# Making the low parts of the middle weight slots on GpSimd instead of VectorE in a two-layer attention/RWKV trunk

## What is computed

```python
for i in range(DEPTH):                       # DEPTH = 2
    p = x @ (w_in0 if i == 0 else w_in_rest[i - 1])
    p_att, p_gate = p[..., :N_ATT], p[..., N_ATT:N_ATT + N_GATE]
    p_rw = token_shift(p[..., N_ATT + N_GATE:N_IN0], mu_rwkv[i])   # r, k, v, w, a, g
    y_a = dsa_sparse_mqa(...)                # attention, 8 heads
    y_b = rwkv7_time_mix(...)                # a scan over time, 16 heads of 64
    g_a, g_b = jnp.split(jax.nn.sigmoid(p_gate + b_gate[i]), 2, axis=-1)
    x = layer_norm(alpha * x + (g_a * y_a + g_b * y_b) @ w_out[i], ...)
    x = layer_norm(alpha * x + conv_glu_ffn(x, ...), ...)
```

## Time and profile before

| | before |
|---|---|
| time, median of 3 runs | 1276.94 us (1275.41 to 1277.79) |
| time of the profiled execution | 1279.3 us |
| its span, first to last instruction | 1277.0 us |
| TensorE busy | 1183.0 us (93%) |
| VectorE, ScalarE, GpSimd busy | 768.0, 541.2, 53.7 us |
| mean granted TensorE clock | 0.981 of full speed |

### The profile page before, as it was taken

How to read it: one execution, slowest core, us unless ns; L and a number is a source line. 1 busy time by engine, 2 the same in 40 slices (tenths; PEclk the granted TensorE clock), 3 DMA queues, 4 the chain that set the end, 5 groups by cost and what they waited for, 6 DMA issues and landing times.

```text
span 1277.0 us, 28992 instructions
## 1 busy us (share of the span) xinstructions
PE 1183.0 (93%) x12328; PEld 1071.2 (84%) x12328; DVE 768.0 (60%) x1368; ACT 541.2 (42%) x954; POOL 53.7 (4%) x56
## 2 busy tenths in 40 slices
PE   7998999999989699999799989989999996999995
PEld 7778897978889599998597878979788996999984
DVE  0268565657457677774512775757584666777744
ACT  1343535354344255653112445354533443555530
POOL 0000000000000100000100000000000001000000
PEclk9999999999999799999999999999999998999998
DMA  7422221211175445555354222212111853555551
GB/s 261 149 87 88 84 87 45 88 51 60 52 250 169 158 157 189 183 195 201 114 193 148 84 75 67 93 52 92 40 47 52 275 174 129 188 180 193 199 187 43
DMA packets 45335, 165.35 MB, mean 129 GB/s; under 512 B 5120, under 2 KB 5376, under 8 KB 44960
## 3 DMA queue, kind: packets, MB, share of 16 engines
q1 hardware_dynamic: 42560, 154.01, 35.4%
q0 software_dynamic: 1504, 7.47, 1.9%
q10 hardware_dynamic: 1152, 2.10, 0.5%
HBM read 160.42 MB, written 3.15 MB: 128 GB/s over the span
## 4 chain that ended last, share of the span: by engine, by line
PE 78%; DVE 13%; ACT 3%; DMA 3%; issue 1%; POOL 1%; SPq 0%; POOLq 0%; DVEq 0%; ACTq 0%
PE ps L690 18%; PE ps L691 16%; PE ps L692 16%; PE ps L823 10%; PE ps L669 5%; PE ps L932 3%; DMA ring<-stream_dram 2%; PE ps L830 2%; DVE ring_r L1391 1%; DVE keep L1772 1%; PE ps L974 1%; DVE small L1770 1%; DVE ln L1635 1%; DVE X_Y L1501 1%; DVE x_tok L1632 1%
## 5 line engine op out<-in xcount | busy, mean ns | idle before, releaser
L690 PE MATMUL ps<-x_tok_r,mid_hi 128*128 128x256 f32 x448 | 137.0, 306 | 8.2 <-DVE ring_r L1391 8.2
L691 PE MATMUL ps<-xT_r,mid_hi 128*128 128x256 f32 x448 | 126.5, 282 | 0.0
L692 PE MATMUL ps<-x_tok_r,ring_r 128*128 128x256 f32 x448 | 126.3, 282 | 0.0
L669 PE MATMUL ps<-xT,ring 128*128 128x256 f32 x448 | 99.7, 381 | 0.0
L690 PEld LDWEIGHTS ps<-x_tok_r,mid_hi 128*128 128x128 f32 x448 | 85.1, 190 | 15.8 <-issue 8.4
L669 PEld LDWEIGHTS ps<-xT,ring 128*128 128x128 f32 x448 | 84.2, 190 | 13.0 <-issue 1.6
L691 PEld LDWEIGHTS ps<-xT_r,mid_hi 128*128 128x128 f32 x448 | 85.5, 191 | 0.0
L692 PEld LDWEIGHTS ps<-x_tok_r,ring_r 128*128 128x128 f32 x448 | 85.4, 191 | 0.0
L1391 DVE TENSOR_TENSOR ring_r<-ring,mid_hi 128x1024 fp32r<-128x1024 f32 x56 | 68.1, 1219 | 14.7 <-ACT mid_hi L1078 14.1
L1614 DVE TENSOR_TENSOR rs_ks_r<-ring,tha_kkn_r 128x1024 fp32r<-128x1024 f32 x46 | 56.4, 1225 | 25.2 <-ACT tha_kkn_r L1113 25.2
L1501 DVE COPY_PREDICATED X_Y<-masks,ps 128x256 f32<-128x256 uint32 x80 | 35.1, 438 | 60.0 <-PE ps L823 60.0
(11 more groups left out here) (427 smaller groups left out, 3361.4 us busy)
## 6 DMA issues: line engine op xcount, KB each, us to landing
ring<-stream_dram SPq DMA_DIRECT2D x281, 512.0 KB, 3.3
lora_w<-lora_dram POOLq DMA_DIRECT2D x2, 1536.0 KB, 7.2
W_bt<-rpar_dram POOLq DMA_DIRECT2D x4, 512.0 KB, 4.7
kt_V<-rpar_dram POOLq DMA_DIRECT2D x4, 512.0 KB, 6.0
x_tok<-x_dram SPq DMA_DIRECT2D x2, 512.0 KB, 4.6
v_saved_dram<-vs_dC ACTq DMA_DIRECT2D x4, 256.0 KB, 3.6
x_tok<-x_dram SPq DMA_DIRECT2D x1, 1024.0 KB, 5.0
vf<-v_saved_dram ACTq DMA_DIRECT2D x4, 256.0 KB, 3.5
```

Source lines behind the costliest of these rows:

```text
L669: mm = pe.matmul(dst[:, b, :], w[:, kb * P:kb * P + P], rhs[:, kb, :], start=(kb == 0), stop=(kb == KB - 1))
L690: pe.matmul(dst, lh, rh, start=start, stop=False)
L691: pe.matmul(dst, lh, rl, start=False, stop=False)
L692: return pe.matmul(dst, ll, rh, start=False, stop=stop)
```

## The change

The low parts of the middle slots are made by GpSimd. The semaphore is `pool_mid` in place of `dve_mid`. GpSimd makes them in the order in which TensorE reads them; its small steps are placed among them by gap: `y_rstd(r - 1)` after the slots of gap 2, `head_norm(r + 1)` after those of gap 13. VectorE's five calls of `mids_up_to` go. TensorE waits for `xr` by itself before middle slot 0.

```diff
@@ gpsimd
+            def mids_up_to(l, end):
+                for m in range(pool_mid.next - l * MID_PER_LAYER, min(end, MID_PER_LAYER)):
+                    k = SLOT_AT[MIDS[l * MID_PER_LAYER + m]] % RING
+                    pool.wait_ge(*act_mid(l, m))
+                    pool.tensor_tensor(rounded["ring"][:, k, :], ring[:, k, :], f32(mid_hi[m % NM][:, :]), ALU.subtract
+                                       ).then_inc(*pool_mid.inc(l, m))
+            def y_rstd(r):
+                pool.wait_ge(*dve_y(r, "v8"))
+                pool.tensor_scalar(g8[:, 3, :], g8[:, 2, :], 1.0 / N_R, GN_EPS, ALU.mult, ALU.add
+                                   ).then_inc(*pool_y.inc(r, "eps"))
+                pool.wait_ge(*pool_y(r, "eps"))
+                pool.tensor_tensor(g8[:, 4, :], g8[:, 3, :], half[:, 0:NU], ALU.pow
+                                   ).then_inc(*pool_y.inc(r, "rstd"))
@@ gpsimd, the rounds
                 for g in range(GROUPS):
                     r = GROUPS * l + g
+                    mids_up_to(l, mids_by(GAPS * g + 2))
+                    if g:
+                        y_rstd(r - 1)
+                    mids_up_to(l, mids_by(GAPS * g + 13))
                     if g + 1 < GROUPS:
                         head_norm(r + 1)
-                    pool.wait_ge(*dve_y(r, "v8"))
-                    pool.tensor_scalar(g8[:, 3, :], g8[:, 2, :], 1.0 / N_R, GN_EPS, ALU.mult, ALU.add
-                                       ).then_inc(*pool_y.inc(r, "eps"))
-                    pool.wait_ge(*pool_y(r, "eps"))
-                    pool.tensor_tensor(g8[:, 4, :], g8[:, 3, :], half[:, 0:NU], ALU.pow
-                                       ).then_inc(*pool_y.inc(r, "rstd"))
+                    mids_up_to(l, mids_by(GAPS * g + 13 + 2 * (NCH - 1)))
+                y_rstd(r)
@@ tensor, pair_pieces
-                        pe.wait_ge(*dve_mid(l, m))
+                        if m == 0:
+                            pe.wait_ge(*dve_parts(l, "xr"))
+                        pe.wait_ge(*pool_mid(l, m))
@@ vector
-            def mids_up_to(l, end):
-                for m in range(dve_mid.next - l * MID_PER_LAYER, min(end, MID_PER_LAYER)):
-                    k = SLOT_AT[MIDS[l * MID_PER_LAYER + m]] % RING
-                    dve.wait_ge(*act_mid(l, m))
-                    dve.tensor_tensor(rounded["ring"][:, k, :], ring[:, k, :], f32(mid_hi[m % NM][:, :]), ALU.subtract
-                                      ).then_inc(*dve_mid.inc(l, m))
@@ vector, grams / level / after grams / after each chunk
-                if r % GROUPS:
-                    mids_up_to(r // GROUPS, mids_by(GAPS * (r % GROUPS) - 1) - 1)
-                mids_up_to(r // GROUPS, mids_by(GAPS * (r % GROUPS) + 2))
-                    mids_up_to(r // GROUPS, mids_by(GAPS * (r % GROUPS) + 1 + 2 * lev + k))
-                    mids_up_to(l, mids_by(GAPS * g + 3))
-                        mids_up_to(l, mids_by(GAPS * g + 13 + 2 * c))
```

More of the change, by code:

```diff
@@ L451, in trunk @@
         act_mid = by_layer("act_mid", list(range(MID_PER_LAYER)))
-        dve_mid = by_layer("dve_mid", list(range(MID_PER_LAYER)))
+        pool_mid = by_layer("pool_mid", list(range(MID_PER_LAYER)))
         mid_last = mid_gaps()
```

## The result

The changed kernel takes 1288.1 us (median of 9 runs, 1285.05 to 1298.68), the kernel before 1277.7 us beside it (9 runs, 1273.16 to 1281.96). The ratio is 1.0088 with an interval of 1.0062 to 1.0113: slower, by 11.2 us, with 7.9 and 14.4 as bounds. Forecast were +3.8 us. The side and the cause (VectorE held while GpSimd subtracts) were as forecast; the size was not.

What follows compares the result with a forecast made beforehand. TensorE, 78% of the chain, plus its waits bounds the kernel. Two layers lose 4.4 us and slot 0 gives -0.6: +3.8 us, median 1280.7 us; the forecast's own range is 1276 to 1290, 8-in-10 range 1265 to 1293.

Steps and rivals of the forecast that it cites:

- Price of a low part: One subtraction on GpSimd was taken as 2.25 us, within bounds of 1.2 and 3.1 us.
- Held both ways: GpSimd's subtraction holds VectorE's operations with two SBUF inputs, just as they hold GpSimd; forecast case at 0.45 chance.
- first rival: VectorE is not held, so only gains remain: -10.9 us, 1266.0 us; chance 0.28.
- Chunks: Chunk 1 of each round and the last round's chunk 2: S held, 0.49 us lost each, 2.45 a layer.
- Level 3: Rounds 1 and 2: subtraction leaves the chain ahead of the second X update, 1.0 us gained twice a layer.
- y_scale: Level 2 of rounds 1 and 2: L1566 held by slot 12's subtraction, 0.2 us lost each, 0.4 a layer.
- starts of rounds 1 and 2: GpSimd's subtraction holds L1480, which TensorE reads 0.3 us late in each of these rounds.
- slot 0 of layer 0: xr starts 1.7 us late, less the 1.15 of the removed subtraction: 0.55 us lost.
- the start of round 3: Held L1480 makes Y start 0.75 us late with no middle slots as cover: 0.75 us lost a layer.
- The clock: Forecast is wrong if TensorE's granted clock falls in the last round's longer pauses; no size in the sum.
- Slot 0 of layer 1: GpSimd is done before xr, so the removed subtraction gains 1.15 us.
- third rival: A low part takes 2.65 us or more and VectorE is held longer: +15 us, 1292, up to 1304; chance 0.10.

Runs made afterwards that it cites:

- fills: Changed kernel with each GpSimd subtraction replaced by two fills of the same tile that read nothing, low parts zero: 1266.74 us, ratio 0.9892.
- one-wait kernel: Changed kernel with GpSimd starting slot 24 only after VectorE is through with akrk of round 3: 1285.83 us, ratio 1.0052 to the kernel before.

## Why the forecast held in sign and not in size

- **Price of a low part.** Taken 2.25 us, measured 2.37. The Trainium skill (GPSIMD Engine Reference, Elementwise — side-by-side cycle accounting) gives 4497 ns for 2048 elements, as an estimate 2.25 us for half; the trace has 5% more. By the forecast's own slope (3.8 us at 2.25, 15 at 2.65) the 0.12 us would have brought 3.4 us more, 7.2 in all. The places do not show it: the ten in the chunks, where a longer subtraction should tell, came out below the forecast.
- **Held both ways.** Shown: S waits for the subtraction's end in all 16 places of the group (chunks 1 and 2), and does not beside fills. The first rival (no holding) is out, and so is its ground, the 1.23 us at 358.97: there GpSimd's instruction reads 8 elements.
- **Chunks.** 0.49 forecast, 0.37 measured: 1.2 us too much over ten places. In chunk 2 of rounds 0 to 2 S is held as well, and the cover that I had named is there: they moved by nothing.
- **Level 3, y_scale, starts of rounds 1 and 2, slot 0 of layer 0.** -0.91 for -1.0, 0.16 for 0.2, 0.32 for 0.3, 0.61 for 0.55. xr now takes 4.06 us from 113.11, by the end of the second subtraction.
- **The step that failed: the start of round 3, put at 0.75 us a layer.** It measured 2.9 in both, without the clock. I followed the held L1480 to its end and let L1486 and Y run behind it at their usual length. But the hold itself moves what follows into the next slot's subtraction: the second half of L1486 waits too, and Y comes about 3 us late. The groups show that this happens at every start: L1495 has 14.7 us more than before ((1398 - 479) ns x 16), which is seven pairs at 2.1 us, the three round starts of each layer and slot 0 of layer 1. In rounds 1 and 2 the middle slots cover it, as I had said; in round 3 there is nothing to cover with. The runs with slot 24, slot 25 and both settle it: by the matmuls 0.82, 0 and 2.94 us a layer. The 0.75 was right for the one hold that I had followed; the hold behind it was missing.
- **The clock.** Named as what could go wrong, and not in the sum. TensorE's products behind the 2.82-us pause run at 0.50 of full clock in layer 0. The two falls in that stretch give away 2.6 us there (1.5 of it right behind the pause, the rest at 320.9) and 1.7 in layer 1. How much of that is the change's stays open. In layer 1 the same pause of 2.82 us is followed by the same products in 1.15 us, at full clock, and the fall comes 1.1 us after they begin; with slots 24 and 25 alone layer 1 has one only 8.4 us after, as the kernel before has. In layer 0 six profiles of kernels without the two holds in a row also have a spell of half clock, 8.6 to 9.9 us after these products begin, and the kernel before and three others have none. So the second fall of layer 0 is not of this change alone; the first, right behind the pause, stands in the two kernels with both holds and in no other. Each kernel was profiled once, and no run here holds the clock fixed.
- **Slot 0 of layer 1, -1.15 forecast.** I had only looked whether GpSimd is done before xr, which it is. Its first subtraction catches L1495 before Y, by the same pair pattern (VectorE's timeline after; the two took 0.88 us before):

```profile
745.69 2.98 DVE L1495 SCALAR_TENSOR_TENSOR tmp<-rs_ks,cpar 128x256 f32<-128x256 f32 x2
748.84 0.74 DVE L1520 COPY_PREDICATED X_Y<-masks,ps 128x512 f32<-128x512 uint32 x1 [0.17 <-PE ps L840]
```

  The gain was there (-1.18 us), and the hold took 1.47 (read in the one-wait kernel's profile, which has no half clock at this place): +0.3, and the rest is a half-clock spell at 744. The kernel in which slot 0 waits for this step has the gain alone.
- **Level 4 of round 0, not in the forecast.** Four tensor_scalar operations of att_norm take 3.16 us beside slot 4 instead of 1.01 (137.79), 0.29 us a layer. I had counted only operations with two SBUF inputs as held.

The sum with these terms: 3.8, + 4.4 for round 3 (2 x 2.2 more), + 1.45 for slot 0 of layer 1, + 0.6 for level 4, - 1.2 for the chunks, + 0.4 for the level 3 gains: 9.4 us before any clock. That lies within the measured 7.9 to 14.4; the 1.8 us to the 11.2 may be clock, or nothing.

That 1288.1 us still lies within the forecast's own 1276 to 1290 is luck in part: the sum was let move with the price of a low part alone, and that price was nearly as taken. By the time alone the third rival (1292 us, at 2.65 us a low part) was nearer to it than the forecast's 1280.7; the measured 2.37 us and the holds in a row speak against that rival.

## What to carry to other kernels

Before work goes to GpSimd, walk along VectorE's queue at each place and ask which instruction meets the new one, then redo the walk from the delayed times, because one hold can push the next instruction into the next hold. Give GpSimd what lies beside VectorE instructions that take one of their inputs from PSUM, and leave it alone where VectorE is dense and TensorE has nothing to fill with: three slots of 28 in the right places gained 5.9 us, all 28 lost 11.2. And a wait of TensorE for one engine is often cured by an earlier place in that engine's queue: the move within VectorE and ScalarE took 4.6 of the 8.2 us of wait without GpSimd.

## What the runs showed of the hardware that was not expected

- A dense queue of VectorE does not keep GpSimd out. The subtraction that begins at 301.09, while L1487 still runs, goes ahead of L1489, which would have followed without a gap; VectorE then waits until it ends. The same at 304.39, between the two halves of L1495.
- A fill of 128x1024 on GpSimd takes 0.95 to 1.01 us and slows no two-input instruction of VectorE in the whole profile (S 0.29 us), but it does slow tensor_scalar with one SBUF tile: four of L1610 take 2.42 us instead of 1.01. In the one-wait kernel even a tensor_scalar of 8 elements took 1.84 us instead of 0.17.
- Of four pauses of TensorE of 2.82 us for this mask (the changed kernel and the one with slots 24 and 25, both layers), the two in layer 0 were followed by products at half clock (32 in 1.97 and 1.84 us), the two in layer 1 by the same products at full clock (1.15 us). So the pause alone does not decide it. Behind a pause of 0.71 us (slot 24 alone) they took 1.15 us.
